# Two value projections as tokens by features: activations as the matmul's weights, against transposes of the result

## The chip, the cores and the metric

The kernel runs on one core of a Trainium2 chip. The metric is the device time of one execution in microseconds (us). A core has five engines that run side by side and meet through semaphores: TensorE (PE, matrix products into the memory PSUM, which has 8 banks of 128 rows by 512 fp32 words), VectorE (DVE), ScalarE (ACT), GpSimd (POOL) and SyncE (SP, which here only issues transfers).

## The reference, cut to what matters

The program is two transformer blocks of two layers each over 512 tokens (x) with 256 context tokens (ctx), 768 in all, width 1024. The part that matters here is how two layers make their values.

```python
# layer 0, gated linear attention (GLA): h = modulated rmsnorm(x), hc the same of ctx
q, k, v, r = split(h @ w_in)            # 512, 512, 1024, 1024 columns; v is 4 heads x 256
...
o_intra = einsum('bnhts,bnshv->bnthv', scores, vc)          # contracts over tokens s
S = S * exp(bl)[..., None] + einsum('bthd,bthv->bhdv', ks, vv)   # contracts over tokens t
# layer 1, latent attention (MLA): c_kv has 256 features per token
kv = (rmsnorm(c_kv, kv_lora_norm) @ w_ukv).reshape(B, L, 8, 128 + 128)
k_nope, v = kv[..., :128], kv[..., 128:]
...
p = softmax(s * 192 ** -0.5)
o = einsum('bhqk,bkhv->bqhv', p, v)                          # contracts over tokens k
```

The values are read with tokens along the contracted axis, so they are wanted in memory as tokens (on the 128 partitions) by features. All arithmetic is fp32.

## The kernel before, in words

Activations lie as features by tokens: a block of 128 features stands on the partitions, 768 tokens (`NT`) along them. A projection (`linear`, L725 is its matmul) takes a weight tile of up to 1024 rows by 128 output columns. Each operand is split in a high and a low part of type fp32r, and for each block of 128 input features it issues three products (high x high, low x high, high x low), each in two pieces of 384 tokens. The 128x128 weight block is what TensorE loads, the tokens stream. A result is features by tokens.

Weight tiles come in one list (`weight_tiles`) and go in that order through a ring buffer: SP loads tile t when `FREED[t]` tiles are done (semaphore `lin_done`), ScalarE makes the high part (`w_hi`), VectorE the low one (`w_lo`). ScalarE and VectorE do that in `ahead()`, called once for each tile and two or three tiles early. Each engine's instructions run strictly in the order in which the code is written; no scheduler moves them.

GLA's input projection is 25 tiles (gate, 8 of q and k, 8 of v, 8 of r). For each value tile, ScalarE copies the 128x768 result out of PSUM, TensorE turns it in six 128x128 transposes (`turn_v`, L808, in plain fp32), and VectorE copies the turned result to the arena as tokens by features. Meanwhile VectorE also works on the modulation vectors of later layers (`modulation`), and SP loads two blocks of 512 KB for these beside each weight tile.

MLA's projections are a list of 28 pieces (`mla_specs`), run by `pipeline`: 20 of kind "norm" (4 rotary and 8 plain query pieces, 8 key pieces), then 8 of kind "turn" for the values. For piece n TensorE runs `linear`, then the second stage of piece n-1 (`stage2`): a sum over partitions (L986) for a norm, six transposes (L989) for a turn. Between them ScalarE squares and copies the result, then takes the inverse root, and VectorE multiplies (`tail_made`).

After the list comes the attention over 32 blocks (8 heads x 4 query blocks). `plain` (L1058) and `rotated` (L1066) make the scores of two blocks, VectorE takes the row maximum (`negated_max`), ScalarE the exponentials (`exps`, with the sum), VectorE divides (`probs`), TensorE turns the probabilities (`turn`, L1076), ScalarE copies them, and TensorE multiplies with the values (`values`, L1086). The first blocks have nothing beside them.

Of the kernel before, what the change touches and what calls it, by code (L numbers as in the profile page):

```python
# [14 lines left out]
P = 128  # L15
# [24 lines left out]
FFN_T = (33, 135)  # L40
PACKED = ((0, 25), (93, 136), (195, 229), (289, 323))
# [122 lines left out]
def weight_tiles():  # L164

    t = [(8, P, lambda g: apart(g["gla_gate_w1"][0, 0], g["gla_gate_w1"][0, 1]))]
    t += [(8, P, lambda g, c=m * P: columns(g["gla_w_in"][0], c)) for m in range(24)]
# [6 lines left out]
    t += [(2, P, lambda g, c=h * 256 + o: columns(g["mla_w_ukv"][0], c)) for o in (0, 128) for h in range(8)]  # L174
# [8 lines left out]
    return t  # L183

# [83 lines left out]
def mla_specs(QN0, QR0, MK0, MV0):  # L268
# [7 lines left out]
    s += [dict(kind="turn", latent="kv", k=2, dmas=1, segs=ALL, dst=MV0 + h * P, pitch=D) for h in range(8)]  # L276
# [19 lines left out]
def build(nc, A, out):  # L296
    ctx = ExitStack()
    with ctx:
# [75 lines left out]
        def lin_at(t, segs, slots, upper=0):  # L374
# [7 lines left out]
            if slots == 4:  # L382
                return PS[:, upper + t % 4, :]
            return PS[:, (upper + 2 * (t - upper)) % 4, :] if upper else PS[:, 2 * (t % 2), :]
# [100 lines left out]
        def halves(ap):  # L485
# [12 lines left out]
            tail_sum tail_rs tail_made rot_in0 rot_in1 kpe_in rope_made down_taken up_taken lat_sq lat_sum kpe_squared cn_done kpe_made  # L498
# [39 lines left out]

        def r_tile(h, v):
            return R0 + (2 * h + v) * NT  # L540
# [33 lines left out]

        def down_latent(m):
            return f_(LC0 + (m * NX if m < 3 else 3 * NX + (m - 3) * NT), NX if m < 3 else NT)
# [4 lines left out]
        MLA_TAILS = 28  # L581
# [119 lines left out]
        def _(pe):  # L701
# [100 lines left out]
            def turn_v(s, behind):  # L802

                pe.wait_ge(*C.at("free_a", lag=behind))
                wait(pe, C.at("vt_done"))
                C.n["vt_done"] += 1
                for t in range(6):
                    last = pe.transpose(flat(2)[:, t * P:(t + 1) * P], T[:, s, t * P:(t + 1) * P], ident)  # L808
                last.then_inc(*C.out("tr_done"))
# [14 lines left out]
            for m in range(2, 24):  # L824
                linear(1, ALL, hi, lo, "free_a", 2)
                if 9 <= m <= 16:
                    turn_v((m - 1) % 2, 1)
                if m == 18:
                    pe.wait_ge(*C.at("vt_done"))
                    pe.wait_ge(*C.next("w2_dma", 16))  # L830
                    decays(0)
# [160 lines left out]
            def pipeline(specs, lin):  # L992

                tail = Tail()
                for n in range(len(specs) + 1):
                    if n < len(specs):
                        lin(n, specs[n])
                    if n >= 1:
# [42 lines left out]
            pipeline(specs, lin)  # L1041
            pe.wait_ge(*C.at("tail_sum", on="tail_made"))
            pe.wait_ge(sems["rope_made"], MLA_ROPES)
            pe.wait_ge(*C.at("free_a"))
# [269 lines left out]
        def _(act):  # L1314
# [207 lines left out]
            for m in range(25):  # L1522
                t = ahead()
                act.wait_ge(*C.at("lin_done"))
# [145 lines left out]
            def latents(n):  # L1670
# [5 lines left out]
                if n == 2:  # L1676
                    latent_high(1)
            for m in range(6):
# [31 lines left out]

            for p in range(18):
                for s in (2 * p, 2 * p + 1):
                    if s < 32:
# [127 lines left out]
        def _(dve):  # L1841
# [254 lines left out]
            Vt = AF[:, V0:V0 + 6 * D].rearrange("p (t v) -> p t v", v=D)  # L2096
# [54 lines left out]
            for t in range(24):  # L2151
# [164 lines left out]
            def latents(n):  # L2316
# [13 lines left out]
                if n == ROPE_LAG:  # L2330
                    dve.wait_ge(*C.next("pc_dma", 16))
                    rotate(KPE0, True)
# [211 lines left out]
```

## Time and profile before

| | us |
|---|---|
| median of 3 runs | 2897.76 (2897.2 to 2900.31) |
| the profiled execution | 2897.56 |
| its span, first to last instruction | 2895.8 |
| TensorE busy | 2838.5 (98%) |
| VectorE busy | 1749.3 (60%) |
| ScalarE busy | 1211.9 (42%) |

The span is cut into 40 slices, each digit a tenth of the slice:

```
PE   8999999999999999999999999999999999999999
DVE  5755758754674454447546468865355488765463
ACT  4225745321333384445324355553233455643231
```

TensorE is busy nearly throughout, so the time is read from what TensorE does or waits for in each stretch. GLA's input projection lies at 25 to 254 us, MLA's projections at 998 to 1114 us, its attention at 1114 to 1258 us. "Busy" of a matmul is a modelled duration in which neighbours overlap; the distance from start to start, and the chain of work that ended last, tell what one costs. PEclk in the rows is the granted clock as a share of 2.4 GHz: 1.00 is 2.4, 0.5 is 1.2.

### The profile page before, as it was taken

Reading aid. Unit: us, or ns where it says so; the run is one execution under the profiler, and the core shown is the slowest. Engines: PE = TensorE matmul, PEld = TensorE weight load, DVE = VectorE, ACT = ScalarE, POOL = GpSimd, SP = SyncE. Lnnn points to the kernel's source line nnn. Section 1 sums busy time; section 2 is a strip of 40 time slices with the busy share of each in tenths; the row PEclk is TensorE's granted clock in tenths of the full one; section 3 lists DMA queues with packets and bytes.
Section 4 is the critical chain, followed back from the end, with each engine's and each line's share of the span. In section 5 each row is a group of like instructions: output and inputs, shape, how many; then the busy total and the mean of one; then the engine's idle time right before and its main releaser. Section 6 shows DMA issues by size and latency. Waiting matters only on the chain.

```text
span 2895.8 us, 37302 instructions
## 1 busy us (share of the span) xinstructions
PE 2838.5 (98%) x14430; PEld 2390.9 (83%) x14430; DVE 1749.3 (60%) x2649; ACT 1211.9 (42%) x1846; POOL 59.0 (2%) x115
## 2 busy tenths in 40 slices
PE   8999999999999999999999999999999999999999
PEld 6998799999999966788888876578888765688887
DVE  5755758754674454447546468865355488765463
ACT  4225745321333384445324355553233455643231
POOL 0000000000000000000000010000000000000000
PEclk9999999999999999999999999999999999999999
DMA  7530023333432110012322231122233221123223
GB/s 287 194 124 30 1 91 119 123 134 105 129 122 71 58 61 28 1 64 94 101 96 95 95 113 66 30 80 95 95 100 106 97 84 48 49 94 107 87 97 107
DMA packets 74352, 266.20 MB, mean 92 GB/s; under 512 B 8912, under 2 KB 12496, under 8 KB 72896
## 3 DMA queue, kind: packets, MB, share of 16 engines
q1 hardware_dynamic: 64224, 230.31, 23.8%
q0 software_dynamic: 9952, 33.50, 3.4%
q8 instruction: 115, 1.88, 0.3%
q14 instruction: 61, 0.50, 0.1%
HBM read 253.55 MB, written 2.10 MB: 88 GB/s over the span
## 4 chain that ended last, share of the span: by engine, by line
PE 86%; DVE 6%; issue 4%; ACT 3%; DMA 0%; SPq 0%; ACTq 0%; DVEq 0%
PE psum L725 75%; DVE arena L1847 2%; ACT temps L1321 2%; DVE row_stats L1847 2%; PE psum L1058 2%; PE psum L1266 1%; PE psum L1204 1%; PE psum L1066 1%; PE psum L1086 1%; ACT arena L1321 1%; DVE temps L1847 1%; DMA w_raw<-in_weights 0%; PE psum L1186 0%; PE psum L1136 0%; PE psum L1253 0%
## 5 line engine op out<-in xcount | busy, mean ns | idle before, releaser
L725 PE MATMUL psum<-arena_r,w_hi 128*128 128x512 f32 (+3 forms) x7736 | 2075.8, 368 | 2.6 <-DVE arena_r L1847 1.8
L725 PEld LDWEIGHTS psum<-arena_r,w_hi 128*128 128x128 f32 x7736 | 1392.7, 188 | 221.6 <-issue 61.5
L725 PE MATMUL psum<-arena_r,w_lo 128*128 128x512 f32 (+4 forms) x3868 | 1260.0, 363 | 0.0
L725 PEld LDWEIGHTS psum<-arena_r,w_lo 128*128 128x128 f32 x3868 | 711.2, 188 | 82.8
L1847 DVE TENSOR_TENSOR w_lo<-w_raw,w_hi 128x1024 fp32r<-128x1024 f32 (+4 forms) x383 | 456.0, 1191 | 497.2 <-ACT w_hi L1321 496.2
L1321 ACT ACTIVATE w_hi<-w_raw 128x1024 fp32r<-128x1024 f32 (+4 forms) x383 | 393.8, 1029 | 518.2 <-DMA w_raw<-in_weights 518.0
L1321 ACT ACTIVATE temps<-temps 128x512 f32<-128x512 f32 (+2 forms) x202 | 132.2, 657 | 150.8 <-DVE temps L1847 148.6
L1847 DVE SCALAR_TENSOR_TENSOR temps<-psum,vectors,temps 128x511 f32<-128x511 f32 x246 | 150.9, 655 | 62.1 <-ACT temps L1321 60.2
L1321 ACT ACTIVATE arena<-psum 128x768 f32<-128x768 f32 (+1 forms) x126 | 90.9, 727 | 166.3 <-PE psum L725 59.3
L1321 ACT ACTIVATE arena_r<-temps 128x512 fp32r<-128x512 f32 (+1 forms) x103 | 70.7, 686 | 143.2 <-DVE temps L1847 143.2
L1847 DVE TENSOR_TENSOR arena_r<-temps,arena_r 128x512 fp32r<-128x512 f32 (+1 forms) x103 | 78.1, 758 | 78.6 <-ACT arena_r L1321 78.6
L1321 ACT ACTIVATE temps<-psum,vectors 128x768 f32<-128x768 f32 (+1 forms) x85 | 75.2, 885 | 112.3 <-PE psum L725 105.1
L1847 DVE SCALAR_TENSOR_TENSOR X<-psum,modulation,X 128x512 f32<-128x512 f32 x72 | 45.4, 658 | 111.6 <-PE psum L725 111.5
L1847 DVE TENSOR_REDUCE row_stats<-psum 128x1 f32<-128x768 f32 (+1 forms) x64 | 69.5, 1086 | 69.0 <-PE psum L1066 55.8
L1847 DVE SCALAR_TENSOR_TENSOR temps<-modulation_weights,vectors,temps 128x511 f32<-128x511 f32 x88 | 66.1, 751 | 40.6 <-ACT temps L1321 39.0
L1321 ACT ACTIVATE temps<-X 128x512 f32<-128x512 f32 (+1 forms) x55 | 39.0, 709 | 123.3 <-DVE X L1847 120.1
L1321 ACT ACTIVATE temps<-psum 128x768 f32<-128x768 f32 (+1 forms) x82 | 54.3, 706 | 68.2 <-PE psum L725 52.7
L1321 ACT ACTIVATE temps<-modulation_weights,vectors 128x512 f32<-128x512 f32 x44 | 36.0, 817 | 85.7 <-DVE modulation_weights L1847 85.7
L1847 DVE CUSTOM_DVE_ANT_0 arena<-arena,vectors 128x1024 f32<-128x1024 f32 x56 | 71.6, 1279 | 0.0
L1321 ACT ACTIVATE temps<-psum,fixed_constants 128x512 f32<-128x512 f32 (+1 forms) x58 | 42.1, 726 | 61.3 <-PE psum L1136 54.2
L1847 DVE SCALAR_TENSOR_TENSOR X<-psum,ones_gate,X 128x512 f32<-128x512 f32 x48 | 35.9, 749 | 39.8 <-PE psum L725 39.8
L671 POOL DMA_DIRECT2D modulation_weights<-arena x60 | 31.7, 532 | 1358.5 <-DVE arena L1847 1358.3
(204 smaller groups left out, 2107.8 us busy)
## 6 DMA issues: line engine op xcount, KB each, us to landing
w_raw<-in_weights SPq DMA_DIRECT2D x259, 512.0 KB, 3.3
w_raw<-in_weights SPq DMA_DIRECT2D x64, 704.0 KB, 4.0
arena<-in_ada SPq DMA_DIRECT2D x32, 512.0 KB, 3.6
arena<-in_ada POOLq DMA_DIRECT2D x24, 512.0 KB, 4.6
modulation_weights<-in_ada POOLq DMA_DIRECT2D x24, 512.0 KB, 3.8
arena<-in_ada_first SPq DMA_DIRECT2D x8, 1024.0 KB, 19.3
w_raw<-in_weights SPq DMA_DIRECT2D x32, 256.0 KB, 2.7
modulation_weights<-arena POOLq DMA_DIRECT2D x60, 128.0 KB, 1.9
```

The costliest lines, as they stand in the source:

```text
L671: pool.dma_start(to[row:P:2, :], AF[1 - row:P:2, dst:dst + NX]).then_inc(*C.out(landed, 16))
L725: last = mm(lin_at(t, segs, slots, upper)[:, s:s + m], w[:, c], x(k, s, m), start=(k == 0 and a == 0), stop=(k == n_k - 1 and a == 2))
L1058: mm(flat(2 + n % 2)[:, a:a + m], f_(QN0 + h * NX + q * P, P), f_(MK0 + h * NT + a, m), start=True, stop=False)
L1066: last = mm(flat(2 + n % 2)[:, a:a + m], AF[rows, QR0 + h // 2 * NX + q * P:QR0 + h // 2 * NX + (q + 1) * P], AF[rows, KPE0 + a:KPE0 + a + ...
L1086: last = mm(PS[:, 2 + h % 2, q * P:(q + 1) * P], VM[:, t, h * P:(h + 1) * P], PT1[n % 4][:, t * P:(t + 1) * P], start=(t == 0), stop=(t == 5))
L1204: last = mm(PS[:, 4 + 2 * (n % 2) + c, :], AF[64 * c:64 * c + 64, QB0 + j * NX + q * P:QB0 + j * NX + (q + 1) * P], AF[64 * c:64 * c + 64, ...
L1266: last = mm(PS[:, 2, rows], VB[:, t, j * P:(j + 1) * P], PTB[:, t, rows], start=(t == 0), stop=(t == 3))
L1321: act.activation(out_, in_, func, **kw).then_inc(*C.out(signal))
L1847: op(*args, **kw).then_inc(*C.out(signal))
```

## The change

Both value projections swap the operands. The normalized activations (a block of 128 features by 128 tokens) are loaded as TensorE's weights, and 512 columns of the projection's weights stream, so that the result is 128 tokens by 512 features, as it is wanted. The arithmetic (three products per block of features) is the same.

- GLA: the 8 value tiles hold other parts of `w_in`: two halves (u) of 512 columns, each in four tiles (c) of two blocks of 128 rows. `values_tile` goes over six blocks of tokens (r), and six results, each in its own PSUM bank, grow over the four tiles of a half. ScalarE copies them out (128x512) after the last of the four. `turn_v`, the copies to `temps` and VectorE's copies are gone.
- MLA: the 8 tiles of 256 rows by 128 columns become 2 of 1024 words a partition; each serves six results of 128 tokens by 512 features (`value_row`, 12 in all, i = 0 to 11). The 8 "turn" pieces leave the list. Rows 0 and 1 stand where the next piece's `linear` stood before the last norm's sum, rows 2 to 5 behind that sum, rows 6 to 11 behind the first two blocks' scores. Even rows are copied out by ScalarE (`v_even`), odd ones by VectorE (`v_odd`).
- The tile list is 6 shorter, and the places in the ring follow: `FREED` of the third tile behind the first value tile (the second of the output projection) is now "the first value tile is done".

```diff
-FFN_T = (33, 135)
-PACKED = ((0, 25), (93, 136), (195, 229), (289, 323))
+FFN_T = (33, 129)
+PACKED = ((0, 25), (93, 130), (189, 223), (283, 317))
+V_T = FFN_T[1] - 10
...
+    t += [(8, P, lambda g, r=c * 2 * P, v=D + u * NX: columns(g["gla_w_in"][0][r:r + 2 * P], v, NX)) for u in range(2) for c in range(4)]
...
-    t += [(2, P, lambda g, c=h * 256 + o: columns(g["mla_w_ukv"][0], c)) for o in (0, 128) for h in range(8)]
+    t += [(2, P, lambda g, c=h * 256: columns(g["mla_w_ukv"][0], c)) for h in range(8)]
+    t += [(8, P, lambda g, u=u: value_columns(g["mla_w_ukv"][0], u)) for u in range(2)]
...
+def value_columns(w, u):
+    return np.concatenate([columns(w, h * 256 + 128) for h in range(4 * u, 4 * u + 4)], axis=1)
...
-    s += [dict(kind="turn", latent="kv", k=2, dmas=1, segs=ALL, dst=MV0 + h * P, pitch=D) for h in range(8)]
...
+        def gla_value_bank(u, r):
+            return PS[:, ((4, 5, 6, 7, 2, 3), (0, 1, 4, 5, 6, 7))[u][r], :]
...
+        def value_bank(i):
+            return PS[:, (2, 3, 0, 1)[i % 4], :]
+        def value_ready(i):
+            return (sems["lin_done"], V_T + 1 + i // 6) if i % 6 == 5 else (sems["v_done"], i + int(i < 5))
+        def value_rows(i):
+            return f_(MV0 + i % 6 * D + i // 6 * NX, NX)
...
-            def turn_v(s, behind):
-                pe.wait_ge(*C.at("free_a", lag=behind))
-                wait(pe, C.at("vt_done"))
-                C.n["vt_done"] += 1
-                for t in range(6):
-                    last = pe.transpose(flat(2)[:, t * P:(t + 1) * P], T[:, s, t * P:(t + 1) * P], ident)
-                last.then_inc(*C.out("tr_done"))
+            def values_tile(u, c):
+                t = C.n["lin_done"]
+                pe.wait_ge(sems["w_lo"], t + 1)
+                for r in range(NTT):
+                    if c == 0:
+                        if u == 0 and r == 4:
+                            pe.wait_ge(*C.at("free_a", lag=1))
+                        if u == 1 and r == 0:
+                            pe.wait_ge(*C.at("free_a"))
+                        if u == 1 and r >= 2:
+                            pe.wait_ge(sems["vt_done"], r - 1)
+                    rows = slice(r * P, (r + 1) * P)
+                    for k in range(2):
+                        w = slice(k * NX, (k + 1) * NX)
+                        h, l = hi(2 * c + k)[:, rows], lo(2 * c + k)[:, rows]
+                        mm(gla_value_bank(u, r), h, w_hi(t)[:, w], start=(c == 0 and k == 0), stop=False)
+                        mm(gla_value_bank(u, r), l, w_hi(t)[:, w], start=False, stop=False)
+                        last = mm(gla_value_bank(u, r), h, w_lo(t)[:, w], start=False, stop=(c == 3 and k == 1))
+                    if r == NTT - 1:
+                        last.then_inc(*C.out("lin_done"))
+                    elif c == 3:
+                        last.then_inc(*C.out("tr_done"))
...
+                if 8 <= m <= 15:
+                    values_tile((m - 8) // 4, (m - 8) % 4)
+                    continue
+                if m in (16, 17):
+                    pe.wait_ge(sems["vt_done"], 6 if m == 16 else 8)
                 linear(1, ALL, hi, lo, "free_a", 2)
-                if 9 <= m <= 16:
-                    turn_v((m - 1) % 2, 1)
...
-            def pipeline(specs, lin):
+            def pipeline(specs, lin, beside):
                 tail = Tail()
                 for n in range(len(specs) + 1):
                     if n < len(specs):
                         lin(n, specs[n])
+                    else:
+                        beside()
...
-            pipeline(specs, lin)
-            pe.wait_ge(*C.at("tail_sum", on="tail_made"))
-            pe.wait_ge(sems["rope_made"], MLA_ROPES)
-            pe.wait_ge(*C.at("free_a"))
+            def value_row(i):
+                t = C.n["lin_done"]
+                if i % 6 == 0:
+                    pe.wait_ge(sems["w_lo"], t + 1)
+                if i < 4:
+                    pe.wait_ge(*C.at("free_a", lag=int(i < 2)))
+                else:
+                    pe.wait_ge(sems["v_odd" if i % 2 else "v_even"], i // 2 - 1)
+                a = CN0 + i % 6 * P
+                for k in range(2):
+                    w = slice(k * NX, (k + 1) * NX)
+                    rows_hi, rows_lo = r_(a + k * NT, P), r_(a + 1536 + k * NT, P)
+                    mm(value_bank(i), rows_hi, w_hi(t)[:, w], start=(k == 0), stop=False)
+                    mm(value_bank(i), rows_lo, w_hi(t)[:, w], start=False, stop=False)
+                    last = mm(value_bank(i), rows_hi, w_lo(t)[:, w], start=False, stop=(k == 1))
+                last.then_inc(*C.out("lin_done" if i % 6 == 5 else "v_done"))
+            def first_values():
+                value_row(0)
+                value_row(1)
+            pipeline(specs, lin, first_values)
...
+            for i in range(2, 6):
+                value_row(i)
+            pe.wait_ge(*C.at("tail_sum", on="tail_made"))
+            pe.wait_ge(sems["rope_made"], MLA_ROPES)
             plain(0)
             plain(1)
             rotated(0)
+            for i in range(6, 12):
+                value_row(i)
             for p in range(18):
                 for s in (2 * p, 2 * p + 1):
+                    if s == 2:
+                        pe.wait_ge(*C.next("v_even", 6))
+                        pe.wait_ge(*C.next("v_odd", 6))
```

ScalarE:

```diff
+                if 9 <= m <= 16:
+                    for r in range(NTT if m in (12, 16) else 0):
+                        act.wait_ge(*(C.next("tr_done") if r < NTT - 1 else C.at("lin_done")))
+                        step(f_(V0 + r * D + (m - 9) // 4 * NX, NX), gla_value_bank((m - 9) // 4, r), ACT.Copy, "vt_done")
+                    continue
...
-                elif m <= 16:
-                    if m >= 11:
-                        act.wait_ge(*C.next("tr_done"))
-                    step(T[:, (m - 1) % 2, :], src, ACT.Copy, "free_a")
...
+                if n == 20:
+                    ahead()
+                    value_row(0)
+            def value_row(i):
+                act.wait_ge(*value_ready(i))
+                step(value_rows(i), value_bank(i), ACT.Copy, "v_even")
...
+            value_row(2)
+            value_row(4)
+            ahead()
+            exps(0)
+            value_row(6)
+            exps(1)
+            value_row(8)
+            value_row(10)
             for p in range(18):
                 for s in (2 * p, 2 * p + 1):
-                    if s < 32:
+                    if 2 <= s < 32:
```

VectorE:

```diff
-                if 10 <= t <= 17:
-                    dve.wait_ge(*C.next("tr_done"))
-                    step(cp, "vt_done", Vt[:, :, (t - 10) * P:(t - 9) * P],
-                         flat(2).rearrange("p (t v) -> p t v", v=P))
...
+                step(cp, "v_odd", value_rows(i), value_bank(i))
...
+            value_row(3)
+            value_row(5)
+            ahead()
+            negated_max(0)
+            negated_max(1)
+            value_row(7)
+            probs(0)
+            value_row(9)
+            probs(1)
+            value_row(11)
+            for p in range(1, 18):
```

Where TensorE's instructions stand at a GLA value tile before: the end of one tile (L725), the transposes of the tile before it (L808), and the next tile.

```order
L725 MATMUL psum<-arena_r,w_hi 128x384 x4
L725 MATMUL psum<-arena_r,w_lo 128x384 x2
L808 MATMUL psum<-fixed_constants,temps 128x128 [waits vt_done,free_a]
L808 MATMUL psum<-fixed_constants,temps 128x128 x5
L725 MATMUL psum<-arena_r,w_hi 128x384 [waits free_a,w_lo]
L725 MATMUL psum<-arena_r,w_hi 128x384 x3
L725 MATMUL psum<-arena_r,w_lo 128x384 x2
```

And now, in the first tile of the second half, where the third block of tokens takes a bank that the first half used (L839 to L841 are the three products; weights and streamed operand have changed places):

```order
L841 MATMUL psum<-w_lo,arena_r 128x512
L839 MATMUL psum<-w_hi,arena_r 128x512 [waits vt_done]
L840 MATMUL psum<-w_hi,arena_r 128x512
L841 MATMUL psum<-w_lo,arena_r 128x512
L839 MATMUL psum<-w_hi,arena_r 128x512
```

The transposes and their waits for `free_a` and the copy are gone; the four waits for `vt_done` of this form stand only in this tile.

TensorE at the end of MLA's projections before: the last value piece, the last two groups of transposes, and the first two blocks' scores up to the first that needs an exponential.

```order
L725 MATMUL psum<-arena_r,w_lo 128x384 x2
L989 MATMUL psum<-fixed_constants,temps 128x128 [waits tail_made,free_a]
L989 MATMUL psum<-fixed_constants,temps 128x128 x5
L989 MATMUL psum<-fixed_constants,temps 128x128 [waits tail_made,free_a]
L989 MATMUL psum<-fixed_constants,temps 128x128 x5
L1058 MATMUL psum<-arena 128x512 [waits free_a,rope_made,tail_made]
L1058 MATMUL psum<-arena 128x256
L1058 MATMUL psum<-arena 128x512
L1058 MATMUL psum<-arena 128x256
L1066 MATMUL psum<-arena 128x512 x2
L1066 MATMUL psum<-arena 128x256 x2
L1058 MATMUL psum<-arena 128x512 [waits e_made]
```

And now (L1118 is `plain`, L1126 `rotated`, L1096 to L1098 a value row's products): the end of row 5, the same scores, and row 6, which stands with five more rows ahead of the first wait for an exponential.

```order
L1096 MATMUL psum<-w_hi,arena_r 128x512
L1097 MATMUL psum<-w_hi,arena_r 128x512
L1098 MATMUL psum<-w_lo,arena_r 128x512
L1118 MATMUL psum<-arena 128x512 [waits rope_made,tail_made]
L1118 MATMUL psum<-arena 128x256
L1118 MATMUL psum<-arena 128x512
L1118 MATMUL psum<-arena 128x256
L1126 MATMUL psum<-arena 128x512 x2
L1126 MATMUL psum<-arena 128x256 x2
L1096 MATMUL psum<-w_hi,arena_r 128x512 [waits v_even,w_lo]
L1097 MATMUL psum<-w_hi,arena_r 128x512
L1098 MATMUL psum<-w_lo,arena_r 128x512
```

ScalarE at the same place now: the last norm's root, rows 2 and 4, the high part of the output projection's second tile, the first exponential, and row 6.

```order
L1390 ACTIVATE temps<-psum,fixed_constants 128x768 [waits tail_rs,tail_sum]
L1390 ACTIVATE temps<-temps 128x768 [waits act_own]
L1390 ACTIVATE arena<-psum 128x512 [waits act_own,v_done]
L1390 ACTIVATE arena<-psum 128x512 [waits tail_rs,v_done]
L1390 ACTIVATE w_hi<-w_raw 128x1024 [waits v_even,w_in2]
L1390 ACTIVATE temps,row_stats<-psum,row_stats 128x768 [waits v_even,nm_made]
L1390 ACTIVATE arena<-psum 128x512 [waits w_hi,v_done]
```

Before, eight copies of 128x768 stood between that root and the first exponential.

## Rows read from the trace of the kernel before

**Rows 1.** The page: busy time of each engine, and its share of the span.
```profile
PE 2838.5 (98%) x14430; PEld 2390.9 (83%) x14430; DVE 1749.3 (60%) x2649; ACT 1211.9 (42%) x1846; POOL 59.0 (2%) x115
```

**Rows 2.** The chain that ended last: start us, us, what.
```profile
63.61 66.81 PE psum L725 x384
130.41 0.66 PE psum L808 x6
...
176.01 8.32 PE psum L725 x48
...
193.32 0.66 PE psum L808 x6
193.97 16.65 PE psum L725 x96
```

**Rows 3.** The same chain, later: a stretch of 512-column matmuls.
```profile
1337.06 326.98 PE psum L725 x1440
```

**Rows 4.** Windows: us, busy of PE, PEld, DVE, ACT, POOL, PEclk, DMA share, GB/s.
```profile
64.00:130.00 66.00, 66.00 (x383) 66.00 (x382) 52.19 (x79) 15.37 (x17) 0.00 (x0) 1.00 0.64 217
130.00:194.00 64.00, 64.00 (x389) 63.74 (x388) 48.40 (x70) 13.54 (x15) 0.00 (x0) 1.00 0.42 140
1112.00:1121.00 9.00, 5.44 (x24) 2.98 (x24) 4.24 (x8) 1.39 (x4) 0.00 (x0) 1.00 0.00 0
1121.00:1126.00 5.00, 5.00 (x12) 2.43 (x13) 1.37 (x3) 0.79 (x2) 0.00 (x0) 0.66 0.00 0
276.00:283.00 7.00, 4.81 (x30) 4.53 (x30) 5.71 (x11) 4.71 (x12) 0.00 (x0) 0.76 0.00 0
```

**Rows 5.** Timeline of PE at the last norms: start, us, instructions, idle before.
```profile
1087.00 1.16 PE L725 MATMUL psum<-arena_r,w_hi 128*128 128x384 f32 x4
...
1090.21 1.56 PE L986 MATMUL psum<-temps,fixed_constants 128*128 128x384 f32 x4 [0.66 <-ACT temps L1321]
```

**Rows 6.** The chain that ended last from the last piece to the first transposed probabilities.
```profile
1106.53 2.09 PE psum L725 x12
1108.62 0.66 PE psum L989 x6
...
1114.18 2.85 PE psum L1058 x8
1117.03 1.51 PE psum L1066 x8
...
1120.79 4.54 PE psum L1058 x8
1125.33 1.51 PE psum L1066 x8
1126.84 0.02 issue
```

**Rows 7.** Timeline of ScalarE and VectorE: the last norm but one.
```profile
1090.98 0.84 ACT L1321 ACTIVATE temps<-temps 128x768 f32<-128x768 f32 x1
...
1091.86 1.02 DVE L1847 SCALAR_TENSOR_TENSOR arena<-temps,vectors 128x768 f32<-128x768 f32 x1 [2.96 <-ACT temps L1321]
```

**Rows 8.** Groups by form, of ScalarE and VectorE: count, busy us, mean ns, idle before.
```profile
L1321 ACT ACTIVATE arena<-psum 128x512 f32<-128x512 f32 x48 | 28.6, 596 | 64.6 <-PE psum L1253 44.9 <-PE psum L1171 19.7
L1321 ACT ACTIVATE w_hi<-w_raw 128x1024 fp32r<-128x1024 f32 x259 | 273.2, 1055 | 299.8 <-DMA w_raw<-in_weights 299.5
L1321 ACT ACTIVATE temps<-psum,row_stats 128x768 f32<-128x768 f32 x32 | 28.9, 902 | 72.2 <-DVE row_stats L1847 72.1
L1847 DVE COPY arena<-psum 128x512 f32<-128x512 f32 x10 | 6.9, 687 | 4.8 <-PE psum L1139 4.8
L1847 DVE TENSOR_TENSOR w_lo<-w_raw,w_hi 128x1024 fp32r<-128x1024 f32 x259 | 316.8, 1223 | 308.8 <-ACT w_hi L1321 307.9
L1847 DVE TENSOR_REDUCE row_stats<-psum 128x1 f32<-128x768 f32 x32 | 30.5, 953 | 55.8 <-PE psum L1066 55.8
```

**Rows 9.** The page, transfers: count, KB each, median us from issue to landing.
```profile
w_raw<-in_weights SPq DMA_DIRECT2D x259, 512.0 KB, 3.3
```

More of the change, by code:

```diff
@@ L166, in weight_tiles @@
     t = [(8, P, lambda g: apart(g["gla_gate_w1"][0, 0], g["gla_gate_w1"][0, 1]))]
-    t += [(8, P, lambda g, c=m * P: columns(g["gla_w_in"][0], c)) for m in range(24)]
+    t += [(8, P, lambda g, c=m * P: columns(g["gla_w_in"][0], c)) for m in range(8)]
+    t += [(8, P, lambda g, r=c * 2 * P, v=D + u * NX: columns(g["gla_w_in"][0][r:r + 2 * P], v, NX)) for u in range(2) for c in range(4)]
+    t += [(8, P, lambda g, c=m * P: columns(g["gla_w_in"][0], c)) for m in range(16, 24)]
     t += [(8, P, lambda g, c=m * P: columns(g["gla_w_out"][0], c)) for m in range(8)]
@@ L382, in lin_at @@
             if slots == 4:
-                return PS[:, upper + t % 4, :]
-            return PS[:, (upper + 2 * (t - upper)) % 4, :] if upper else PS[:, 2 * (t % 2), :]
+                return PS[:, upper + (t - FFN_T[1] + 3) % 4, :]
+            return PS[:, (2 * t - upper - FFN_T[1] + 3) % 4, :] if upper else PS[:, 2 * (t % 2), :]
         def raw(t):
@@ L497, in build @@
             state_done upd o_done o_taken sq_made on_made ot_done ot_taken gated u_made silu_made prod_made act_hi act_ready
-            tail_sum tail_rs tail_made rot_in0 rot_in1 kpe_in rope_made down_taken up_taken lat_sq lat_sum kpe_squared cn_done kpe_made
+            tail_sum tail_rs tail_made rot_in0 rot_in1 kpe_in rope_made down_taken v_done v_even v_odd up_taken lat_sq lat_sum kpe_squared cn_done kpe_made
             nm_made e_made p_made tp_done pt_made pv_done y_hi y_done od_made
@@ L580, in build @@
         MLA_ROPES, ROPES, ROPE_LAG = 5, 13, 4
-        MLA_TAILS = 28
+        MLA_TAILS = 20
         KPE_TURNED = f_(8448, NX)
@@ L824, in _ @@
             for m in range(2, 24):
+                if 8 <= m <= 15:
[3 more added lines that the diff above has]
+                    pe.wait_ge(sems["vt_done"], 6 if m == 16 else 8)
                 linear(1, ALL, hi, lo, "free_a", 2)
-                if 9 <= m <= 16:
-                    turn_v((m - 1) % 2, 1)
                 if m == 18:
-                    pe.wait_ge(*C.at("vt_done"))
+                    pe.wait_ge(*C.next("vt_done", 2 * NTT))
                     pe.wait_ge(*C.next("w2_dma", 16))
@@ L2095, in _ @@
                     split_to(3)
-            Vt = AF[:, V0:V0 + 6 * D].rearrange("p (t v) -> p t v", v=D)
             def log_gates(h):
@@ L2332, in latents, with value_row @@
                     rotate(KPE0, True)
+                if n == 20:
+                    ahead()
+                    value_row(1)
+            def value_row(i):
+                dve.wait_ge(*value_ready(i))
+                step(cp, "v_odd", value_rows(i), value_bank(i))
             for m in range(6):
@@ L2362, in _ @@
             C.n["sc_done"] = 3 * GH
-            for p in range(18):
+            value_row(3)
+            value_row(5)
+            ahead()
+            negated_max(0)
[6 more added lines that the diff above has]
+            for p in range(1, 18):
                 ended = 2 * (p // 4 - 1) if p > 4 and p % 4 == 1 else None
```

## The prediction

> **What bounds the kernel now.** I read the page's busy times first: TensorE is busy 98% of the span, the other engines 60% and less [rows 1]. So what takes work off TensorE shortens the run nearly one for one, and what only takes work off ScalarE or VectorE brings nothing, unless TensorE waits for it. Then the chain that ended last. From 63 to 210 us it is TensorE alone: tiles of 48 matmuls, and six transposes (L808) after each of eight of them [rows 2]. The windows over 64 to 194 us say the same: PE busy throughout, granted clock 1.00 [rows 4]. In MLA the eight value pieces are also bound by TensorE: 2.09 us of matmuls and 0.66 of transposes each [rows 6]. Then comes a place where TensorE does wait: the first two blocks' scores go from 1114.18 to 1118.54, VectorE and ScalarE need until 1120.79 for the first exponential, and the next scores follow at a low clock [rows 4, 6]. Those are the three things that the change touches.
>
> **GLA's values, matmuls.** Columns streamed are the same: before 8 tiles x 48 x 384, now 8 x 36 x 512, both 147,456. What differs is the number of matmuls. 384 of 384 columns took 66.81 us, 174.0 ns each [rows 2]; 1440 of 512 columns took 326.98 us, 227.1 ns each [rows 3]. Before: 384 x 0.1740 = 66.8 us. Now: 288 x 0.2271 = 65.4. Gain 1.4 us. Divided by the columns, both fit 1/2.4 GHz plus 14 ns a matmul. The operands change places (activations loaded, projection weights streamed); no row shows that pairing, but both sides are 128x128 fp32r loaded and fp32r streamed either way, so I take the row's price. Bounds: with no fixed part at all (213 ns) it would gain 3.9 us more; with twice the 14 ns (241) the gain would turn into a loss of 2.6.
>
> In the Trainium skill, "TensorE: Matmul & The Clock Gate", section "Back-to-back issue gap", a matmul at full clock costs N/2.4 plus 2.5 ns. The rows show 14 ns instead of 2.5. By the page, 120 fewer matmuls (both projections) would bring 0.3 us and not 1.7, and the time would come out 1.4 us longer than the sum below. I go by the rows.
>
> **GLA's values, transposes.** Eight groups at 0.66 us each on the chain [rows 2] vanish: 5.3 us. VectorE's copy of each and ScalarE's copy of each went beside TensorE; taking them away is worth nothing. What is new: 12 copies of 128x512 on ScalarE, 0.60 us each [rows 8]. In the last tile of a half a result is ready every 6 x 0.2271 = 1.36 us, so ScalarE keeps up, and the last copy ends about 0.7 us behind the tile. The four waits in the second half's first tile ask for copies that were finished in the tile before; so were those that the first two tiles of the r projection wait for. Behind the waiting copies ScalarE queues the high part of later weight tiles: it is held during one tile, and the tile that it then splits is needed two tiles later, some 16 us. Weights and modulation blocks come as before, three transfers of 512 KB a tile, now every 8.2 us instead of 9.0. The tiles from 64 to 130 us ran at 8.35 us with the same load and VectorE at 52 of 66 us without holding TensorE [rows 4]. So nothing is to be paid here. GLA: 1.4 + 5.3 = 6.7 us.
>
> **MLA's values and the start of its attention.** Here I lay the path of TensorE out twice, from the last norm's sum, released by ScalarE at 1090.21 [rows 5], to the first transposed probabilities at 1126.84 [rows 6].
>
> Before that sum the change puts rows 0 and 1 in place of one piece's `linear`. They start as it did at 1087.00 [rows 5] and, with 0.25 us in which the sum before still drains, take 12 x 0.2271 + 0.25 = 3.0 us: to 1090.0, before ScalarE lets the sum start. Hidden with 0.2 us to spare. The bigger weight tiles (1024 columns to split instead of 256) make ScalarE's split 1.06 us instead of 0.40 [rows 5, 7, 8]; it lies in the 1.1 us in which ScalarE waits for VectorE's product of 1.02 us [rows 7], so it just fits.
>
> Now:
> - the last norm's sum, 1090.21 to about 1091.6 [rows 5]
> - rows 2 to 5: 24 x 0.2271 = 5.45, to 1097.05
> - scores of blocks 0 and 1: 2.85 + 1.51 = 4.36 [rows 6], to 1101.4
> - rows 6 to 11: 36 x 0.2271 = 8.18, to 1109.6
> - scores of blocks 2 and 3: 4.36, to 1113.95, and then the first transposes.
>
> Against 1126.84 this is 12.9 us earlier. It holds 5.3 for eight groups of transposes and 0.3 for 24 fewer matmuls (96 x 0.174 against 72 x 0.2271), 1.7 for the slow clock (4.54 instead of 2.85 for the same eight matmuls [rows 6]), and the rest is waiting that the value rows now fill.
>
> Does each wait on the way hold? Row 4 needs row 0 out of its bank: ScalarE ends the root before at 1091.8 [rows 7] and copies until 1092.4; row 4 starts at 1094.3. Row 5 needs row 1: VectorE ends its product at 1092.9, splits a tile (1.22), copies (0.69) [rows 8], 1094.8; row 5 starts at 1095.7. The scores need the last norm: root until 1094.3, product until 1096, against 1097.05. The tightest is the next weight tile: its place in the ring is free only when row 5 is done, 1097.05. Plus 3.3 for the transfer [rows 9], 1.06 and 1.22 for the two splits [rows 8] is 1102.6, and only then can VectorE take the first maximum, 1.2 us later than the scores allow. Maximum 0.95 and a small step 0.15, exponential 0.90 [rows 8]: 1104.7, then row 6's copy, 1105.3. Row 10 wants that bank at 1106.8, and the scores of block 2 want the exponential at 1109.6. So it costs nothing, with 1.5 us to spare. From 1113.95 on the attention runs as it did from 1126.84: the same waits, the same chain. Later stages keep their places in the ring modulo the six missing tiles, so they shift.
>
> **Sum.** 6.7 + 12.9 = 19.6 us off the profiled execution's 2897.56 (0.2 under the median): 2878 us, a span of 2876.2.
>
> **The clock.** The granted clock was 0.66 over 1121 to 1126 us, after 9 us in which TensorE was busy for 5.44, and 0.76 over 276 to 283 us, where TensorE was busy for 4.81 of 7 us [rows 4]. These are half-rate pieces (1.2 GHz) within a stretch at 2.4. With the waits filled I expect no such piece at the attention's start. The one in GLA may fall elsewhere, since everything behind 130 us moves by up to 6.7 us: gone is 1 to 1.7 us better, another one 1.7 worse.
>
> **Rivals.**
> A. A slow piece of clock stays at the attention's start or comes in another gap of GLA: each costs what 4.54 - 2.85 shows, 1.7 us. 2879.7, with two 2881.4. For it: TensorE still waits about 2 us for the exponentials of blocks 2 and 3. Against: there was no slow piece in the rest of the span. Chance 0.14.
> B. The late weight tile. If the transfer takes 10 us instead of 3.3, ScalarE and VectorE stand behind it with two maxima, two exponentials and the copies of rows 6 and 7, and TensorE waits 10 - 3.3 - 1.5 = 5 us: 2883. For it: both engines run in order, and the tile can't start earlier. Against: nothing else is being transferred there, 0 GB/s [rows 4]. Chance 0.10.
> C. The filling fails: the first blocks' softmax ends no earlier relative to the last score, because VectorE and ScalarE now carry twelve copies there. Then MLA brings only its 5.6 us of TensorE work: 2897.6 - 6.7 - 5.6 = 2885. Against: both engines were busy only 4.24 and 1.39 of 9 us there [rows 4]. Chance 0.05.
> D. Slower than before. The new loops change PSUM bank every 3 or 6 matmuls, and if TensorE pauses at each change and the clock falls to 1.2 GHz in them, a matmul costs up to 454 ns instead of 227. All 360: 82 us, 2960. It decides from 19.6 / 0.227 = 86 matmuls at half rate. Against: the loops run dense, and the clock was 1.00 where TensorE had no gaps [rows 4]. Chance 0.02. The skill's page "TensorE: Matmul & The Clock Gate", section "A second HAM failure mode: psum-queue depth-cycling", tells of such a loss at 512 columns; the trace before has no loop that changes bank that often.
> E. The swap doesn't do what it says: with activations as the loaded side the load is not hidden. The loads are 83% of the span beside the matmuls now [rows 1]; a price of 281 ns instead of 227 would eat all the gain. Chance 0.02.
>
> **Numbers.** Forecast 0.67, A 0.14, B 0.10, C 0.05, D and E 0.04. The forecast's own range is 2876.3 (GLA's slow piece gone) to 2879.2. With A and B the range is 2875.5 to 2883.5. 0.2% is 5.8 us, about what a measurement can tell from no change. Every case but D and E ends below 2892: faster 0.95, within 0.2% 0.02, slower 0.03.
>
> **What would show it.** The chain should have L839 to L841 from the ninth tile on without a transpose, 288 matmuls in 65 to 66 us. The stretch from the end of the q and k tiles to the first decays (L816) should be 6.7 us shorter. The first transposed probabilities should start near 1107 us (1113.95 - 6.7). The windows there should show a clock of 1.00 and next to no idle PE before them. 227 ns for a value matmul is right, 240 and more wrong. TensorE idle ahead of row 10 or 11, released by ScalarE or VectorE, would mean B. A gap in the GLA tiles for `vt_done` or `w_lo` would prove the cover wrong.

## The result and the profile after

The changed kernel takes 2878.59 us (median of 4 runs, 2877.1 to 2879.39), the one before 2899.03 on the same chips (2897.2 to 2900.49): a ratio of 0.9929, 95% interval 0.9912 to 0.9946. The forecast was 2878, with 2875.5 to 2883.5 as the range. The profiled execution took 2879.39 us, its span is 2877.6: 18.2 us under the span of before, where the sum said 19.6.

The page of the changed kernel, busy times as in [rows 1]:

```profile
PE 2825.0 (98%) x14214; PEld 2366.2 (82%) x14214; DVE 1738.6 (60%) x2633; ACT 1208.8 (42%) x1842; POOL 59.0 (2%) x115
```

TensorE has 216 instructions fewer (120 matmuls and 96 transposes) and is as full as before. The busy times of the other engines hardly move, as expected: their work was beside TensorE's.

The chain that ended last, at the GLA projection, where [rows 2] stood (start us, us, what): six tiles of q and k (288 matmuls of 384 columns), the first value matmuls, then three tiles of r.

```profile
64.02 50.16 PE psum L746 x288
114.18 0.23 PE psum L839
114.41 0.24 PE psum L840
114.64 0.23 PE psum L841
...
179.50 24.99 PE psum L746 x144
204.49 1.50 PE psum L852 x6
```

From 114.18 to 179.50 are 65.32 us for 288 value matmuls of 512 columns: 226.8 ns each. The 384-column matmuls that they replace took 174.0 ns each, and there were 384 of them. There is no transpose and no gap. From the first of these rows to L852 (the first decays) are 140.47 us; before, from 63.61 to 210.62, it was 147.01. That is 6.54 us.

The windows, columns as in [rows 4]: the value tiles, two places in the GLA heads behind them, each of which holds a piece at half the clock, and the 20 us that end in the first transposed probabilities.

```profile
114.00:179.00 65.00, 65.00 (x289) 53.83 (x288) 48.21 (x72) 15.66 (x20) 0.00 (x0) 1.00 0.52 172
270.00:280.00 10.00, 7.89 (x52) 6.62 (x52) 7.06 (x12) 6.35 (x19) 0.00 (x0) 0.83 0.00 0
295.00:305.00 10.00, 7.81 (x53) 7.01 (x54) 10.00 (x16) 8.20 (x19) 0.00 (x0) 0.83 0.00 0
1089.00:1109.00 20.00, 20.00 (x86) 13.77 (x85) 9.65 (x17) 5.40 (x10) 0.00 (x0) 1.00 0.16 53
```

In the last window TensorE is busy for all 20 us at a clock of 1.00. Before, the same stretch (1107 to 1127 us) had a mean clock of 0.91 and 3.6 us of idle:

```profile
1107.00:1127.00 20.00, 16.44 (x74) 10.56 (x73) 9.49 (x15) 5.22 (x8) 0.00 (x0) 0.91 0.07 24
```

The chain there, now (it answers to [rows 6]): last norm's sum, rows 2 to 5, scores, rows 6 to 11, scores.

```profile
1085.05 1.55 PE psum L1025 x4
...
1092.09 2.58 PE psum L1118 x8
1094.67 1.49 PE psum L1126 x8
...
1104.55 2.58 PE psum L1118 x8
1107.13 1.51 PE psum L1126 x8
```

From the sum to the first transposed probabilities (start 1108.55) are 23.5 us where 36.5 stood. The weight tile whose transfer can't start before row 5 is done comes late, as forecast, and costs nothing. The rows show ScalarE's part of its split, then VectorE's part and the first maximum, with the idle time before them:

```profile
1095.29 1.06 ACT L1390 ACTIVATE w_hi<-w_raw 128x1024 fp32r<-128x1024 f32 x1 [3.93 <-DMA w_raw<-in_weights]
1096.38 1.23 DVE L1933 TENSOR_TENSOR w_lo<-w_raw,w_hi 128x1024 fp32r<-128x1024 f32 x1 [3.56 <-ACT w_hi L1390]
1097.52 0.95 DVE L1933 TENSOR_REDUCE row_stats<-psum 128x1 f32<-128x768 f32 x1
```

The scores were there at 1096.2; VectorE starts on them at 1097.5. TensorE works on value rows meanwhile and waits for nobody.

The table has stretches of all the profiled executions, from start to start of TensorE's instructions, in us. "Heads" is from the first turned keys of GLA to its last turned output. "Attention's start" is from the last of the four matmul records of the last norm's sum (1.1 us behind the first, from which the 23.5 and 36.5 us above are counted) to the first transposed probabilities. "Slow" counts the pieces at a granted clock of 0.5 in the heads and at the attention's start.

| kernel | to the first decays | heads | slow in heads | attention's start | slow there | span |
|---|---|---|---|---|---|---|
| before | 210.5 | 102.7 | 1 | 35.4 | 1 | 2895.8 |
| the change | 204.4 | 103.6 | 2 | 22.4 | 0 | 2877.6 |
| the change again | 203.6 | 102.6 | 1 | 22.5 | 0 | 2875.8 |
| GLA only | 203.9 | 103.8 | 2 | 35.5 | 1 | 2890.3 |
| MLA only | 211.0 | 102.7 | 1 | 22.4 | 0 | 2883.3 |
| rows ahead | 203.5 | 102.5 | 1 | 24.7 | 0 | 2877.7 |
| rows ahead again | 203.6 | 102.6 | 1 | 24.8 | 0 | 2878.0 |
| half columns | 207.6 | 102.7 | 1 | 22.6 | 0 | 2880.1 |
| split later | 203.6 | 102.7 | 1 | 22.4 | 0 | 2875.7 |
| row moved | 204.7 | 103.5 | 2 | 21.1 | 0 | 2876.4 |
| row moved again | 204.6 | 103.7 | 2 | 21.1 | 0 | 2876.3 |
| kept busy | 203.8 | 102.0 | 0 | 22.4 | 0 | 2875.4 |
| both | 204.4 | 102.1 | 0 | 21.1 | 0 | 2874.6 |
| both again | 204.7 | 102.1 | 0 | 21.1 | 0 | 2874.8 |

### The profile page after: what moved, and what is told of

Same layout as the page of the kernel before. It is cut to its first block, busy times and chain, and to the rows that moved or that the text cites. A ratio compares the mean times of both kernels' runs of the same rounds, so it can differ in the third digit from the quotient of the medians.

```text
span 2877.6 us, 36797 instructions
## 1 busy us (share of the span) xinstructions
PE 2825.0 (98%) x14214; PEld 2366.2 (82%) x14214; DVE 1738.6 (60%) x2633; ACT 1208.8 (42%) x1842; POOL 59.0 (2%) x115
## 4 chain that ended last, share of the span: by engine, by line
PE 87%; DVE 6%; issue 4%; ACT 3%; DMA 0%; SPq 0%; ACTq 0%; DVEq 0%
PE psum L746 73%; DVE arena L1933 2%; ACT temps L1390 2%; DVE row_stats L1933 2%; PE psum L1118 2%; PE psum L1335 1%; PE psum L1273 1%; PE psum L1126 1%; PE psum L1146 1%; PE psum L840 1%; PE psum L841 1%; PE psum L839 1%; ACT arena L1390 1%; DVE temps L1933 1%; PE psum L1255 0%
## 5 line engine op out<-in xcount | busy, mean ns | idle before, releaser
L746 PE MATMUL psum<-arena_r,w_hi 128*128 128x512 f32 (+1 forms) x7416 | 2006.0, 369 | 2.9 <-DVE arena_r L1933 2.2
L746 PEld LDWEIGHTS psum<-arena_r,w_hi 128*128 128x128 f32 x7416 | 1337.7, 188 | 221.5 <-issue 61.5
L746 PE MATMUL psum<-arena_r,w_lo 128*128 128x512 f32 (+1 forms) x3708 | 1219.6, 364 | 0.0
L746 PEld LDWEIGHTS psum<-arena_r,w_lo 128*128 128x128 f32 x3708 | 682.8, 188 | 82.5
L1390 ACT ACTIVATE arena<-psum 128x768 f32<-128x768 f32 (+1 forms) x144 | 101.6, 711 | 190.6 <-PE psum L746 61.6
L1933 DVE TENSOR_TENSOR temps<-temps 128x768 f32<-128x768 f32 (+1 forms) x44 | 36.3, 825 | 35.4 <-ACT temps L1390 35.4
```

The costliest lines, as they stand in the source:

```text
L746: last = mm(lin_at(t, segs, slots, upper)[:, s:s + m], w[:, c], x(k, s, m), start=(k == 0 and a == 0), stop=(k == n_k - 1 and a == 2))
L1390: act.activation(out_, in_, func, **kw).then_inc(*C.out(signal))
L1933: op(*args, **kw).then_inc(*C.out(signal))
```

## The experiments

Twelve runs on three chips, four to a chip. The kernel before had medians of 2898.52, 2896.86 and 2897.57 us there, so that medians are compared within a chip alone.

**GLA only.** The kernel before with the GLA part of the diff alone (`values_tile`, its tiles of `gla_w_in` and ScalarE's copies); MLA's eight "turn" pieces stay.

> Only GLA's values swapped; MLA as before. My sum: 1.4 us of matmuls and 5.3 of transposes, 6.7 us under before, 2891 to 2892. In the trace of the whole change the GLA heads behind the projection took 0.95 us longer, with one half-rate piece of clock more; if that comes with the shift of 6.5 us and not by chance, this kernel shows it too and is 5.7 us under before, its heads again 0.9 longer. Rival (the copies of ScalarE or the weights hold TensorE somewhere): under 5 us.

2891.21 us against 2898.52, 7.3 us less (ratio 0.9975, 0.9966 to 0.9985). The projection's stretch is 6.6 us shorter and the heads 1.1 longer, with two slow pieces. The sum for this part holds. The profiled execution is the slowest of the nine runs (2892.22) and the only one with a mean clock of 0.997, the others have 0.998; so the second piece is probably not in each run, which only a trace of the others could show. At the attention's start the slow piece and the waits of before are back:

```profile
1106.00:1115.00 9.00, 5.66 (x27) 2.97 (x24) 3.88 (x5) 1.46 (x3) 0.00 (x0) 1.00 0.00 0
1115.00:1121.00 6.00, 5.77 (x16) 2.87 (x16) 1.74 (x6) 1.17 (x4) 0.00 (x0) 0.72 0.00 0
```

**MLA only.** The changed kernel with the GLA part taken back.

> Only MLA's values swapped; GLA as before. My sum: 12.9 us under before, about 2885 to 2886. The half-rate piece at the attention's start is gone, the clock there 1.00. Rival (only TensorE's removed work counts, 5.6 us): 2892. Second rival (the clock's pieces move at random): the difference scatters by 1.7 us between runs.

2884.91 us, 13.6 less than before (0.9954, 0.9942 to 0.9967), within 1.5 us over five runs. The attention's start is 13.0 us shorter, with no slow piece. So the first rival (5.6 us) is out. The two parts add within the scatter: 7.3 + 13.6 = 20.9, against 20.4 for the whole in the first measurement and 20.0 on the third chip.

**All rows ahead of the scores.** It takes away the work that filled the wait for the first exponential and leaves the swap.

```diff
-            for i in range(2, 6):
+            for i in range(2, 12):
                 value_row(i)
...
             rotated(0)
-            for i in range(6, 12):
-                value_row(i)
```

ScalarE's and VectorE's copies follow the same order.

> The whole change, but with all twelve value rows ahead of the first scores, so that nothing lies between the first scores and the first exponential. Theory (filling): TensorE waits again about 2.3 us for the first exponential, slower than the change by 2.3 us, and by 4.0 if the half-rate piece comes back with the gap. Rival (the filling is worth nothing, TensorE's removed work is the gain): equal to the change within 0.5 us.

2879.89 us. TensorE's timeline shows the wait again, before the scores of blocks 2 and 3. The two windows, columns as in [rows 4], are the 9 us up to it and the 5 us behind:

```profile
1100.62 1.56 PE L1126 MATMUL psum<-arena 64*128 64x512 f32 x8
1104.45 2.85 PE L1118 MATMUL psum<-arena 128*128 128x512 f32 x8 [2.27 <-ACT temps L1388]
1095.00:1104.00 9.00, 7.18 (x30) 4.45 (x28) 4.25 (x6) 2.14 (x3) 0.00 (x0) 1.00 0.19 60
1104.00:1109.00 5.00, 4.55 (x19) 2.40 (x20) 2.12 (x7) 1.39 (x4) 0.00 (x0) 1.00 0.00 0
```

The wait is 2.27 us as in the kernel before, and the stretch is 2.3 us longer than in the change. The half-rate piece did not come back. So the wait is worth 2.3 us, and the slow piece did not follow this one gap alone. Before, gaps of 0.24, 1.05 and 2.27 us stood within 9 us, in which TensorE was busy for 5.44 us [rows 4]; here it is one gap and 7.18 us. Two of the three in the kernel before:

```profile
1114.18 2.85 PE L1058 MATMUL psum<-arena 128*128 128x512 f32 x8 [1.05 <-DVE arena L1847]
1120.79 4.54 PE L1058 MATMUL psum<-arena 128*128 128x512 f32 x8 [2.27 <-ACT temps L1321]
```

The change had not been run on this chip, so the kernel was run again beside it:

> All twelve rows ahead of the first scores, as in the third experiment. Theory (filling): the trace again has 2.3 us of idle TensorE before the first exponential, and on one chip the median is 2.3 us above the change. Rival: within 0.5 us of it; the 1.3 us seen across two batches were the true size.

2880.53 us against 2877.6 for the change on that chip: 2.9 more. The rival (within 0.5 us of the change) is out; the 0.6 us beyond 2.3 lie within the scatter (2879.8 to 2882.39, and 2877.41 to 2879.82).

**Half columns.** The swap, with each GLA value product in two pieces of 256 columns.

```diff
-                        mm(gla_value_bank(u, r), h, w_hi(t)[:, w], start=(c == 0 and k == 0), stop=False)
...
+                        for n, (a, b) in enumerate(((h, w_hi(t)), (l, w_hi(t)), (h, w_lo(t)))):
+                            for s in (0, NX // 2):
+                                last = mm(gla_value_bank(u, r)[:, s:s + NX // 2], a, b[:, k * NX + s:k * NX + s + NX // 2],
```

> The whole change, but GLA's value products streamed in two pieces of 256 columns: 576 matmuls and weight loads instead of 288, the same columns. Theory (512 columns cost 213 + 14 ns, a fixed part per matmul): 288 x 13.6 = 3.9 us slower than the change, 120 ns a matmul. Rival one (the fixed part is 2.5 ns, the page of the skill; TensorE: Matmul & The Clock Gate, Back-to-back issue gap): 0.7 us slower. Rival two (loads of activations as weights are not hidden behind 107 ns of streaming, loads last 188 ns by the trace): at least 174 to 188 ns a matmul, 35 to 43 us slower.

2881.85 us. The chain that ended last has the six tiles before, the values and three tiles of r:

```profile
63.48 50.16 PE psum L746 x288
113.64 69.11 PE psum L841 x576
182.75 24.97 PE psum L746 x144
```

69.11 us for 576 matmuls are 120.0 ns each, 3.8 us more than 65.32: the fixed part is 13.3 ns at 256 columns and 13.5 at 512. Both rivals are out. Most loads last 188 to 192 ns here and yet one comes every 120 ns, so they overlap each other as well as the matmuls.

**Split later.** `ahead()` for the late tile stands behind `exps(1)` on ScalarE and behind `probs(1)` on VectorE.

> The whole change, but the split of the output projection's second tile (whose transfer can't start before value row 5 is done) stands behind the first two exponentials on ScalarE and behind the first two divisions on VectorE. Theory (the late tile is covered, with 1.5 us to spare): the first maximum starts 1 to 3 us earlier, TensorE's path is the same, time equal to the change within 0.5 us. Rival B of the prediction (TensorE waits behind it): faster by over 0.5 us.

2877.41 us, 19.5 under before on its chip, where the change itself wasn't run, so that the medians can't be set side by side. The trace decides: the first maximum is no longer held, and the stretch at the attention's start is 22.4 us as in the change. The late tile costs nothing. Here the scores end at 1094.3 us and VectorE's maximum follows:

```profile
1094.46 0.96 DVE L1933 TENSOR_REDUCE row_stats<-psum 128x1 f32<-128x768 f32 x1 [3.39 <-PE psum L1126]
```

**One row moved.** Row 11 stands behind the first transposed probabilities, in another bank, and VectorE copies it between two divisions.

```diff
-            for i in range(6, 12):
+            for i in range(6, 11):
...
                     if 2 <= s < 34:
                         turn(s - 2)
+                    if s == 2:
+                        value_row(11)
```

> The whole change, but the last value row (12 matmuls' worth of 6, 1.36 us) stands behind the first transposed probabilities, where TensorE waits 1.47 us for the third exponential, and takes another bank. Theory (what fills a wait is free): 1.4 us faster than the change, 2877.2; the idle before that score falls to about 0.1 us. Rival (VectorE's copy of this row between two divisions delays the next blocks): equal to the change within 0.5 us.

2876.91 us. TensorE's timeline has the transposes, the row, and the score that waited 1.47 us in the change (first row, from the change's trace) and now follows without a wait:

```profile
1110.89 1.56 PE L1118 MATMUL psum<-arena 128*128 128x512 f32 x4 [1.47 <-ACT temps L1390]
...
1107.32 0.87 PE L1136 MATMUL psum<-fixed_constants,temps 128*128 128x128 f32 x6
1107.95 0.47 PE L1096 MATMUL psum<-w_hi,arena_r 128*128 128x512 f32 x1
...
1109.19 0.40 PE L1098 MATMUL psum<-w_lo,arena_r 128*128 128x512 f32 x1
1109.66 1.56 PE L1118 MATMUL psum<-arena 128*128 128x512 f32 x4
```

The stretch is 1.3 us shorter, as it must be with a row less in it. What counts is that nothing behind it got longer: from the first transposed probabilities to the end are 1769.1 us in the change and 1769.1 here, with the row in it. Again, beside the change:

> The last value row behind the first transposed probabilities. The stretch from the last norm's sum to those is 1.3 us shorter in the trace; if it is kept to the end, 1.3 us under the change on one chip. Rival (given back by the half-rate pieces): within 0.5 us of it.

2877.15 us against 2877.6: 0.45 less, where the trace says 1.3, and the runs of the two overlap (2876.34 to 2878.88, and 2877.41 to 2879.82). The profiled executions on this chip aren't alike: this one has a second slow piece in the heads (1.0 us) and reaches the first decays 1.0 us later (204.6 against 203.6), both ahead of the moved row. Against the first profiled execution of the change, which has both too, the span is 1.3 us shorter (2876.3 against 2877.6). The next two experiments take the slow pieces out and settle it in the medians.

**Kept busy.** 13 transposes of a constant that nobody reads, in each of the last three `turn_keys`.

```diff
+                if h >= 1:
+                    for t in range(13):
+                        pe.transpose(work(0)[:, 0:P], ident, ident)
                 for d in range(2):
                     pe.wait_ge(*C.next("ks_made"))
```

> The whole change, with 13 transposes of a constant (1.4 us of work that nobody reads) on TensorE ahead of each of the last three turns of a GLA head's keys, where it idles 2.2 us. Theory (the half-rate pieces of the clock in the heads follow this idle time, and each costs 0.6 to 1.0 us): no such piece in the heads, their stretch from the first turned keys to the last turned output falls from 102.5 to 103.6 us to about 102, and the runs scatter less; 2877 to 2878. Rival (the pieces come from something else, or cost nothing): pieces still there, stretch the same or longer by up to 1.4 us a head where the transposes reach past the idle time.

2877.22 us, within 0.9 over five runs. There is no slow piece in the heads, and they take 102.0 us. The timeline shows the filling (L880) and the keys' transposes (L884); the window holds all the heads:

```profile
269.17 1.58 PE L880 MATMUL psum<-fixed_constants 128*128 128x128 f32 x13
271.53 1.74 PE L884 MATMUL psum<-fixed_constants,arena 128*128 128x128 f32 x12 [0.77 <-DVE arena L1936]
...
294.62 1.64 PE L880 MATMUL psum<-fixed_constants 128*128 128x128 f32 x13 [1.26 <-ACT modulation_weights L1393]
296.09 1.47 PE L884 MATMUL psum<-fixed_constants,arena 128*128 128x128 f32 x12
248.00:352.00 104.00, 96.82 (x616) 83.14 (x617) 81.31 (x134) 70.59 (x159) 0.00 (x0) 1.00 0.02 6
```

By the table, one slow piece costs 0.6 us in this stretch (102.6 against 102.0) and a second 1.0 more. All five runs have a mean clock of 0.999, where the change's nine have 0.997 or 0.998.

**Both.** The moved row and the constant's transposes.

> The moved row and the constant's transposes together. If both theories hold the gains add: 1.4 and 0.6 to 1.6 us, 2876 us. If only the row's holds, 2877.2.

2876.0 us, the lowest median of its chip: 1.2 less than with the transposes alone and 0.9 less than with the moved row alone. No run of this kernel (2875.23 to 2876.36) reaches one of the transposes alone (2876.84 to 2877.74). So with no slow piece in the heads of either profiled execution, the medians show what the trace says of the moved row (1.2 and 1.3 us).

> The moved row and the constant's transposes. 1.3 and 0.6 to 1.6 us, so 1.9 to 2.9 under the change on one chip, no half-rate piece in the heads. Rival: no more than the moved row brings.

2875.78 us (2875.34 to 2876.59) against 2877.6 (2877.41 to 2879.82) for the change: 1.8 less, and no run of the one reaches the other's. The forecast was 1.9 to 2.9. It is 1.4 less than the moved row alone on this chip, which speaks against the rival (no more than the row brings), though the runs of these two overlap by 0.25 us.

**The change again**, for comparison with the three runs above on one chip.

> The change itself, on one chip with the next three, since the difference of the runs of before between two chips (1.7 us) is as large as what is told apart here. 19 to 20.5 us under before. Its heads of GLA have one or two half-rate pieces of clock.

2877.6 us, 20.0 under before. Its profiled execution has one slow piece in the heads where the first had two, and a span of 2875.8 us, 20.0 below that of before: the sum's 19.6 is met within 0.4 us where the piece is not doubled.

## Why the prediction was right

**GLA's matmuls.** Forecast 227.1 ns a matmul, measured 226.8. The price of a 512-column matmul holds with activations loaded and weights streamed. The 2.5 ns a matmul of the Trainium skill, "TensorE: Matmul & The Clock Gate", section "Back-to-back issue gap", which the page calls the gap of an isolated single matmul, does not hold for these fp32r matmuls with a load before each: 13.5 ns at 512 columns in the change and 13.3 ns at 256 in the half-column run.

**GLA's transposes and the cover.** Forecast 6.7 us for the projection, measured 6.54 in the profile and 6.6 for GLA alone. No wait for `vt_done` or `w_lo` shows: 65 of 65 us busy.

**MLA.** Forecast 12.9 us, measured 13.0 (12.9 in the change's second execution, where the stretch is 22.5 us instead of 22.4). The terms agree within 0.3 us each, with signs that cancel: the sum took 1.55 us (1.4 in the forecast), rows 2 to 5 5.5 (5.45), the scores 4.1 both times (4.36), rows 6 to 11 8.4 (8.18). The filling of the first exponential's wait, 2.3 us, is shown by taking it away. The 1.7 us of slow clock are shown gone. That they go with the gaps is shown as far as the piece was there in both executions with the old order and in none of the twelve with value rows there; one gap of 2.3 us alone didn't bring it back, and which of the other gaps it needs wasn't tried.

**The clock in GLA (rival A).** This is what the sum lacks. The forecast took the clock in the heads as before; the profiled execution has a second slow piece there: 103.6 us instead of 102.7. The prediction priced a piece at 1.7 us, from matmuls that follow each other without a gap; here it measured 0.6 and 1.0, since the heads also wait for VectorE and ScalarE and part of a piece falls in idle time. Forecast and rival A are both true in part: the same kernel ran once with one piece and once with two. With 0.4 us of slower start (the first full tiles begin at 64.02 instead of 63.61), the terms close: 19.6 - 0.4 - 0.2 - 0.9 + 0.1 = 18.2 us. The term of the clock was missing from the likeliest sum and too large in the rival.

The rival's "no slow piece in the rest of the span" overlooked the start, where the clock is at 0.5 too (a mean of 0.88 over the first 1 to 30 us before). This slow stretch ends at another time in each execution, and the same code reaches the first decays at 203.5 to 204.7 us. It also tells the two kinds of execution apart. The clock over 29.8 to 30.2 us was 0.50 in all four that had a second piece in the heads and 1.00 in the seven that had one; for the change, first and second execution:

```profile
29.80:30.20 0.40, 0.40 (x3) 0.40 (x2) 0.40 (x2) 0.00 (x0) 0.00 (x0) 0.50 0.98 410
29.80:30.20 0.40, 0.40 (x4) 0.40 (x3) 0.40 (x2) 0.00 (x0) 0.00 (x0) 1.00 1.13 471
```

In the four, the first piece begins 23.9 to 24.2 us behind the first turned keys, in the seven 22.7 to 23.4. So a second piece goes with the time at which the clock rises and not with the program; what sets that time is not shown. One of the three executions with useless transposes had 0.50 there as well, and no piece in the heads.

So it is partly luck that the median lies within 0.6 us of the forecast: the two profiled executions of the changed kernel differ by 1.8 us (0.8 up to the first decays, 1.0 in the heads), and the saving is 18.2 us by the first pair of spans, 20.4 by the medians.

**The late tile (rival B).** The mechanism was there, the price nothing. Taking it away left the stretch at 22.4 us.

**Rivals C, D, E.** ScalarE and VectorE carried the copies: busy 5.40 and 9.65 us in the window of 20. The clock was 1.00 in the new loops, which change bank every six matmuls (a change every three, as the prediction has it, doesn't occur), so the loss of the Trainium skill's section "A second HAM failure mode: psum-queue depth-cycling" didn't come. Loads stayed hidden: 226.8 ns a matmul, not 281.

## What to carry to other kernels

If a result is wanted turned, let the activations be the side that is loaded: the product then comes out turned, with the same columns streamed, and the transposes and one of two copies go. Where TensorE is the bound, its removed work is a fair sum, but look as well for a place where TensorE waits for a chain of other engines: matmuls that depend on nothing there are free, and moving them into the wait was worth 2.3 us in the trace and 2.9 in the medians, of some 20 us here. Short idle times of TensorE can cost twice, by the wait and by a slower clock behind it (1.7 us with dense matmuls, 0.6 to 1.0 in a stretch with waits). How often that happened differed between executions, so it is priced as a scatter. And a small gain is told from this scatter by comparing executions with the same slow pieces, as the moved row shows.

## What the runs showed of the hardware that was not expected

- The half-rate pieces of TensorE's clock are no property of the kernel alone: the same program had one in the GLA heads in one execution and two in another, 1.0 us apart. With each of three idle times of 2.2 to 2.3 us in the heads filled by 1.5 us of useless transposes, there was none in three executions. The five runs each lay within 0.9, 1.1 and 1.3 us, where the change's lay within 2.4; but two kernels without the filling were as close (split later 0.8 over four runs, half columns 1.1), so a smaller scatter is not shown.
- 128x128 fp32r loads that last 188 to 192 ns each came every 120 ns without holding up the matmuls: the fixed part of a matmul was the same with 256 columns (13.3 ns) as with 512 (13.5).
